# Modulation weights in pieces of two k-tiles by 512 columns, multiplied by c and added onto an accumulator in PSUM

## The reference, cut to what matters

```python
c_act = jax.nn.silu(c)
for i in range(2):
    mod = (c_act @ ada_w[i] + ada_b[i])[:, None, :]      # ada_w[i] is 1024 x 6144
    sh1, sc1, g1, sh2, sc2, g2 = jnp.split(mod, 6, axis=-1)
    h = rmsnorm_2(x, norm1_g[i]) * (1.0 + sc1) + sh1
    ...
```

## Time and profile before

| | |
|---|---|
| median of 3 runs | 3760.74 us (3753.86 to 3760.88) |
| span of the profiled execution | 3739.3 us, 40173 instructions (its time with what lies around the span is not listed) |
| PE (TensorE matmul) busy | 3177.2 us, 85% |
| DVE (VectorE) busy | 2209.4 us, 59% |
| POOL (GpSimd) busy | 2107.5 us, 56% |
| ACT (ScalarE) busy | 733.7 us, 20% |
| chain that ended last, by engine | PE 59%, DVE 21%, DVEq 9%, issue 5% |
| mean granted TensorE clock | 0.916 of full speed |
| HBM | 255.92 MB read, 69 GB/s over the span |

### The profile page before, as it was taken

One profiled execution on the slowest core, in us unless ns is written; L12 is line 12 of the kernel. 1 busy time (PEld: TensorE's weight loads), 2 busy tenths in 40 slices (PEclk: granted clock), 3 DMA queues, 4 the chain that ended last, 5 costly groups with the idle time before them and its releaser, 6 DMA issues.

```text
span 3739.3 us, 40173 instructions
## 1 busy us (share of the span) xinstructions
PE 3177.2 (85%) x14739; PEld 2448.1 (65%) x14739; DVE 2209.4 (59%) x2245; ACT 733.7 (20%) x1069; POOL 2107.5 (56%) x926
## 2 busy tenths in 40 slices
PE   7886898999779877778777998999989786699998
PEld 6775898789337755566665644677767544467776
DVE  5675654232332497777787554588338667538841
ACT  2253222432330001000000354111010111111100
POOL 5551322765018854566665502688867454368985
PEclk9897999999889987888888999999999898899999
DMA  3110000222002334444444100233222100023332
GB/s 101 56 57 29 1 0 0 79 75 72 0 0 89 120 113 129 117 116 127 132 135 121 57 0 12 79 90 90 93 66 78 59 28 15 23 68 90 90 100 69
DMA packets 365367, 259.46 MB, mean 69 GB/s; under 512 B 6330, under 2 KB 362263, under 8 KB 365005
## 3 DMA queue, kind: packets, MB, share of 16 engines
q1 hardware_dynamic: 361568, 248.53, 22.3%
q0 software_dynamic: 2256, 6.55, 0.6%
q10 hardware_dynamic: 1436, 2.96, 0.2%
HBM read 255.92 MB, written 2.10 MB: 69 GB/s over the span
## 4 chain that ended last, share of the span: by engine, by line
PE 59%; DVE 21%; DVEq 9%; issue 5%; ACT 3%; POOL 2%; POOLq 1%; DMA 1%; ACTq 0%
PE ps L487 13%; PE ps L488 13%; PE ps L489 13%; DVE adw L750 6%; DVEq L749 4%; DVE cv L1863 3%; PE ps L1364 2%; PE ps L1440 2%; PE ps L1344 2%; PE ps L1137 1%; PE ps L1150 1%; PE ps L578 1%; DVEq L2293 1%; PE ps L1247 1%; DVE SG L2247 1%
## 5 line engine op out<-in xcount | busy, mean ns | idle before, releaser
L659 POOL TENSOR_TENSOR spl<-raw,ones 128x1024 fp32r<-128x1024 f32 (+1 forms) x352 | 927.2, 2634 | 813.2 <-PE ps L489 732.3
L487 PE MATMUL ps<-HNH,spl 128*128 128x512 f32 (+1 forms) x2496 | 940.4, 377 | 121.2 <-DVE HNL L591 28.5
L661 POOL TENSOR_TENSOR spl<-raw,spl 128x1024 fp32r<-128x1024 f32 (+1 forms) x352 | 940.4, 2672 | 52.8 <-issue 3.8
L488 PE MATMUL ps<-HNL,spl 128*128 128x512 f32 (+1 forms) x2496 | 914.7, 366 | 0.0
L489 PE MATMUL ps<-HNH,spl 128*128 128x512 f32 (+1 forms) x2496 | 910.7, 365 | 0.0
L487 PEld LDWEIGHTS ps<-HNH,spl 128*128 128x128 f32 x2496 | 492.2, 197 | 243.2 <-issue 94.2
L488 PEld LDWEIGHTS ps<-HNL,spl 128*128 128x128 f32 x2496 | 493.1, 198 | 71.0 <-issue 4.3
L489 PEld LDWEIGHTS ps<-HNH,spl 128*128 128x128 f32 x2496 | 490.6, 197 | 74.0
L750 DVE TENSOR_TENSOR adw<-adw 128x512 f32<-128x512 f32 x192 | 266.8, 1390 | 14.3
L487 PE MATMUL ps<-AFH,spl 128*128 128x512 f32 x528 | 216.6, 410 | 5.3 <-issue 4.2
L2144 DVE SCALAR_TENSOR_TENSOR H<-ps,mod,H 128x512 f32<-128x512 f32 x32 | 24.0, 751 | 323.1 <-PE ps L489 323.1
(11 more groups left out here) (424 smaller groups left out, 5042.1 us busy)
## 6 DMA issues: line engine op xcount, KB each, us to landing
adw<-in_ada_w SPq DMA_DIRECT2D x96, 512.0 KB, 4.1
raw<-in_w_in SPq DMA_DIRECT2D x44, 1024.0 KB, 5.2
raw<-in_ffn_w_up SPq DMA_DIRECT2D x88, 512.0 KB, 4.7
raw<-in_w_ffn_in SPq DMA_DIRECT2D x44, 512.0 KB, 5.3
raw<-in_ffn_w_down SPq DMA_DIRECT2D x16, 1408.0 KB, 6.4
raw<-in_hy_w_in SPq DMA_DIRECT2D x12, 1024.0 KB, 5.1
raw<-in_w_ffn_out SPq DMA_DIRECT2D x8, 1408.0 KB, 7.7
raw<-in_w_branch_dn SPq DMA_DIRECT2D x8, 1024.0 KB, 5.1
```

Source lines behind the costliest of these rows:

```text
L487: pe.matmul(dst, w[0], x[0], start=first, stop=False)
L488: pe.matmul(dst, w[0], x[1], start=False, stop=False)
L659: pool.tensor_tensor(hi, w, heads_of(ones[:, :], gm.kt), ALU.mult)
L661: pool.tensor_tensor(lo, w, hi, ALU.subtract).then_inc(split_ready, 1)
```

## The change

A unit is now a piece of two k-tiles by 512 columns, again 512 KB, and four units in a row (a block) make up four columns of `mod`: 128 partitions x 8 k-tiles x 512 columns. For each of the two k-tiles VectorE does one instruction over 512 elements: it multiplies the weights by one value of silu(c) per partition and adds them onto an accumulator in PSUM (bank 5 or 7, in turn); the block's first only multiplies, and its last writes the sum to `ads` in SBUF. TensorE reduces four times 128 columns at the end of a block, behind one wait. VectorE waits for the reduction of two blocks before ahead of the block's last instruction. VectorE's loop over the slabs of `ffn_in` is written out (`turns_of`), those of the other engines stay loops. `ads` has two buffers of 512 elements in place of four of 128.

```diff
-        adw = fresh("adw", 2, KD, P)
-        ads = fresh("ads", 4, P)
+        adw = fresh("adw", 2, 2, SEQ)
+        ads = fresh("ads", 2, SEQ)
...
+        def turns_of(gm):
+
+            return [(n, range(min(R, gm.nslab - n * R))) for n in range(-(-gm.nslab // R))]
...
-        ada_w = A["ada_w_2"].rearrange("l (k p) n -> l p k n", p=P)
+        ADA_K = 4
+        ADA_BLOCKS = ADA // ADA_K
+        ada_w = A["ada_w_2"].rearrange("l (q k p) n -> l q p k n", p=P, q=ADA_K)
...
         def ada_load(sp, i, c):
 
+            j, q = c // ADA_K, c % ADA_K
             if c >= 2:
-                sp.wait_ge(ada_sum, i * ADA_TURN + (c - 1))
-            sp.dma_start(adw[:, c % 2, :, :], ada_w[c % 2][:, :, ds((i * (ADA_TURN // 2) + c // 2) * P, P)]).then_inc(ada_in[c % 2], 16)
+                sp.wait_ge(ada_used, i * ADA_TURN + (c - 1))
+            sp.dma_start(adw[:, c % 2, :, :], ada_w[j % 2, q, :, :, ds((i * (ADA_TURN // 8) + j // 2) * SEQ, SEQ)])\
+                .then_inc(ada_in[c % 2], 16)
 
         def ada_dve(dve, i, c):
 
+            j, q = c // ADA_K, c % ADA_K
+            acc = ps[:, 5 + 2 * (j % 2), :]
             dve.wait_ge(ada_in[c % 2], i * (16 * ADA_TURN // 2) + 16 * (c // 2 + 1))
-            dve.wait_ge(ada_red, i * ADA_TURN + (c + 1))
-            w = adw[:, c % 2, :, :]
-            dve.tensor_tensor(w, w, wide(csil[:, :]), ALU.mult)
-            for n in (4, 2):
-                dve.drain()
-                dve.tensor_tensor(w[:, 0:n, :], w[:, 0:n, :], w[:, n:2 * n, :], ALU.add)
-            dve.drain()
-            dve.tensor_tensor(ads[:, c % 4, :], w[:, 0, :], w[:, 1, :], ALU.add).then_inc(ada_sum, 1)
+            for h in range(2):
+                k = 2 * q + h
+                w, scale = adw[:, c % 2, h, :], csil[:, k:k + 1]
+                if k == 0:
+                    ins = dve.tensor_scalar(acc, w, scale, None, ALU.mult)
+                else:
+                    dve.drain()
+                    if k == KD - 1:
+                        dve.wait_ge(ada_red, i * (ADA_TURN // ADA_K) + (j + 1))
+                    ins = dve.scalar_tensor_tensor(ads[:, j % 2, :] if k == KD - 1 else acc, w, scale, acc, ALU.mult, ALU.add)
+            ins.then_inc(ada_used, 1)
 
         def ada_pe(pe, i, c):
 
-            pe.wait_ge(ada_sum, i * ADA_TURN + (c + 1))
-            n = i * (ADA_TURN // 2) + (c % 2 * 6 * KD + c // 2)
-            pe.matmul(ps[:, 4, ds(n, 1)], ads[:, c % 4, :], ones[:, 0:1], start=True, stop=True).then_inc(ada_red, 1)
+            if c % ADA_K == ADA_K - 1:
+                j = c // ADA_K
+                pe.wait_ge(ada_used, i * ADA_TURN + (c + 1))
+                for m in range(4):
+                    n = i * (ADA_TURN // 2) + (j % 2 * 6 * KD + j // 2 * 4 + m)
+                    mm = pe.matmul(ps[:, 4, ds(n, 1)], ads[:, j % 2, m * P:(m + 1) * P], ones[:, 0:1], start=True, stop=True)
+                mm.then_inc(ada_red, 1)
...
-            for i, slabs in groups(dve, ffn_in):
+            for i, slabs in turns_of(ffn_in):
                 for r in slabs:
                     for c in ada_units(ffn_in, r):
                         ada_dve(dve, i, c)
```

More of the change, by code:

```diff
@@ L353, in build @@
         ada_in = [sem(f"ada_in{r}") for r in range(2)]
-        ada_sum, ada_red = sem("ada_sum"), sem("ada_red")
+        ada_used, ada_red = sem("ada_used"), sem("ada_red")
         wab_split, n_y, n_hi = sem("wab_split"), sem("n_y"), sem("n_hi")
@@ L994, in _ @@
             pe.sem_inc(vt_ready, 4)
-            pe.sem_inc(ada_red, 4)
+            pe.sem_inc(ada_red, 2)
             pe.sem_inc(l2_sum, 2)
@@ L2166, in _ @@
             add_residual(ffn_out, before=lambda t: with_ada(ffn_out, t))
-            dve.wait_ge(ada_red, 4 + ADA)
+            dve.wait_ge(ada_red, 2 + ADA_BLOCKS)
             dve.tensor_tensor(mod[:, :, :].rearrange("p l n -> p (l n)"), ps[:, 4, 0:ADA], cols("ada_b", 0, ADA), ALU.add)
```

## The result

| | before | after |
|---|---|---|
| median of the runs, us | 3758.72 (3753.86 to 3760.88, 4 runs) | 3544.67 (3535.97 to 3557.47, 4 runs) |
| profiled execution, span | 3739.3 | 3534.9 |
| mean granted clock | 0.916 | 0.938 |
| VectorE busy in the five stages, us | 614.1 | 342.4 |

The ratio is 0.9433, 95% interval 0.9403 to 0.9463. The forecast was 3555, range 3528 to 3632.

A forecast was written before the change was run, and what follows sets the result against it. VectorE, taking turns with GpSimd, was held to set the pace in the five GEMM stages. Span 3739.3 less 206.0 saved there plus 21.4 around it gave 3555 us, range 3528 to 3632.

The forecast's parts named there:

- turns with GpSimd: In the five GEMM stages, VectorE instructions with two SBUF inputs and GpSimd's splits run one at a time, not together.
- rival 1: New products: PSUM as output does not free VectorE from the turns; 77 us more, 3632; chance 0.10.
- 130 to 160: Sign of being right: the new VectorE instructions are busy for 130 to 160 us in place of 472.
- rival 2: TensorE's clock stays at 0.86 in three GEMMs (ffn_in, ffn_out, mix_out); 53 us more, 3608; chance 0.06.
- Pieces done at 38: gate_sb: VectorE finishes the last two pieces 38 us into the stage.
- 21 us for the splits: gate_sb, after the pieces: 16 split instructions, 5 behind GpSimd at 2.6 us and 11 at 0.69.
- 2 us for late pieces: ffn_out: pieces that come late add 2 us to the stage's forecast of 133.
- The reductions: TensorE's reductions of units stay: 44 units add 9 or 10 us in ffn_in, 24 add 5 in ffn_out.
- rival 3: Loads: only one piece is under way, 10.0 us each; 182 us more, 3943; chance 0.05 with others on its side.
- TensorE's wait for four pieces, VectorE's for the reduction: At block ends: TensorE's 24 waits and VectorE's wait for the reduction of two blocks before cost nothing.
- 21.4 us "around the span": Whole kernel: the median of the runs before lay 21.4 us above the profiled span, and this was kept.
- The model of the turns: Own times of instructions taking turns, added per slab or tile: ffn_in 356 us, where 370.2 was measured before.

The follow-up runs named there:

- e1: The changed kernel with its accumulator in SBUF in place of PSUM, and one wait moved: 3668.82 us, ratio 0.9777.
- e2: The kernel before, its pieces and waits kept, but each unit done as eight products of 128 columns onto PSUM: 3579.96 us, ratio 0.9544.
- e7: The changed kernel with branch_sb's product and sum written to PSUM, where the split reads them: 3527.59 us, ratio 0.9414.
- e4: The changed kernel, loading only 32 of a piece's 512 columns from the third piece on: 3544.82 us, ratio 0.946.
- e6: The changed kernel with the eight splits of QSK moved in between gate_sb's pieces, two per slab: 3531.07 us, ratio 0.9415.
- e8: The changed kernel with the edits of e5, e6 and e7 together: 3474.72 us, ratio 0.9266.
- e5: The changed kernel with the first two convolution taps of both conv FFNs kept in PSUM bank 5: 3504.42 us, ratio 0.9345.
- e3: The kernel before, with TensorE's reductions in ffn_in one slab later: 3737.82 us, ratio 0.9955.

## Why the prediction was right

*The cause.* VectorE set the pace by its turns with GpSimd, and the products leave the turns because their accumulator lies in PSUM. e1 and e2 show it from both sides: the place of the accumulator is worth 124 us of 214 when taken away from the new arithmetic, and 179 when given to the old pieces. The two add to more than 214 because the new arithmetic also shortens the turns where they stay. That PSUM as an output alone is enough, which no row of before showed, L759 shows (739 to 754 ns, where the same instruction into SBUF in e1 went up to 3444): rival 1 falls. The Trainium skill, "SBUF — State Buffer", section "Who interferes with whom", has the rule that a VectorE instruction with at most one SBUF input and outside the two-port modes does not contend with GpSimd; all 192 of the new instructions agree (at most 757 ns), e1's 192 in SBUF show the other case (up to 3568 ns).

*The new instructions.* Taken at 0.75, measured 0.747 to 0.755; 144.6 us busy for "130 to 160".

*The stages.* The forecast for each and what it took: gate_sb 59, 56.7; branch_sb 57, 59.7; mix_out 63, 60.7; ffn_in 260, 258.7; ffn_out 133, 131.1. In all 206.0 less was forecast and 211.1 came. To take TensorE as the next bound, and to size it by the same GEMM elsewhere, was right to 1 or 2 us in ffn_in and ffn_out. TensorE's clock came back in both large stages (0.99 and 1.00): rival 2 falls. Some of the small misses have names, that of mix_out (2.3) has none:
- branch_sb was 2.7 over: TensorE waited twice at a block's end, 3.9 and 3.5 us, for pieces that stood behind blocked instructions (e7: gone, 48.1). The prediction had the turns of L2131 and the split, but not that they delay the reduction.
- gate_sb was right by steps that were in part right. Pieces done at 38: they were done 37.4 us in (1291.97 less 1254.6). 21 us for the splits: 19. That the last pieces are late by SP's order was in the text; that the size of the load matters was not so (e4: a sixteenth of the bytes, 0.3 us).
- ffn_out's 2 us for late pieces are not shown: e4 gains 1.7, but e6 to e8 with whole loads take 129.9 to 130.0 as well, and so differ from the kernel after by 1.2 without touching this stage.
- The reductions were added up slightly low: 44 units at 0.24 are 10.6 us, not 9 or 10, and 24 are 5.8, not 5.

*Loads and rival 3.* A piece landed in 5.0 us in the median, under the 6.0 from which the slower case would decide, and two were under way. e4 shows that the bytes have no price here, with 3.5 us of landing left.

*TensorE's wait for four pieces, VectorE's for the reduction.* 7.4 us and none, as costed, but for branch_sb.

*The mis-sized terms.* First the 21.4 us "around the span". In the profiled execution after, 2.2 us lie outside the span (3537.13 and 3534.9), and 2.2 to 3.3 in each of the other runs. The 21.4 was not time around the span: the profiled execution of before was a quick one among runs that spread (3737.64 to 3766.87 in 13 later ones). After, the median is 9.8 above the profiled span. So the term was 11.6 too large. The forecast span was 3533.3, 1.6 below the measured one, and the two together make the median's forecast 10.0 too high. That the forecast is this close owes something to luck: the stages differ by up to 2.7 us in both directions.
Second, what no step named. Outside the five stages the profiled run lost 6.7 us of its gain (3739.3 less 3534.9 is 204.4, not 211.1): the part ahead of them ended 6.1 us earlier, and the first conv FFN took 11.9 longer (fc_in 267.6, fc_out 135.3, for 265.2 and 125.8). The table shows the same GEMMs at two lengths, 125.8 or 134 to 135, 259 or 265 to 271, in kernels that do not differ there, before's included. In e5, without turns in that place, both conv FFNs have one length (250.0 and 250.1, 125.0 and 124.9) and the runs lie within 0.3%. The long fc_out has a sign: TensorE waits 7.1 us for AFL at its start and the clock is 0.96 to 0.97 (the kernel after, e1, e3, the second block of e2), where the short one has 0.5 us of that wait and 1.00, and e5 none. So VectorE's last splits come late there, and the turns are the likely reason, since they and the unevenness go together in e5. A profile of one run can hold 10 us of it. What tips it, and why the first part ended between 1250 and 1261 us in kernels that are alike there, stays open.

*The model of the turns.* The sum of own times gave before's 370 as 356, and the right order of things. It is not a way to size a case: e1 was forecast at 300 to 315 in ffn_in and took 353.4, because the sum leaves out the time in which both engines wait for TensorE. One split for each VectorE instruction that takes part, while GpSimd has work, is what the order of time shows. In the forecast the error sits in branch_sb (55 by this sum), and in rival 1's price, 311 for ffn_in and 3632 in all: e1, whose products do take turns, took 3669, so the upper end of the range was too low for the case that it stood for. The rest of the forecast did not hang on it, as the products no longer take part in any turn.

## What to carry to other kernels

Where VectorE and GpSimd both work from SBUF, look at the longest and shortest time of each VectorE line: here a factor of three and more at one shape was a turn lost. A PSUM bank as accumulator or stopover ended that in four kernels (the change, e2, e5, e7) for every instruction moved there. The price of the turns goes by the number of such instructions, up to the number that GpSimd has to do beside them, and not by their lengths; and what the stage then takes has to be followed through TensorE as well. A wait that names a line (here the reduction, 144 us) says who was late, not what is lost: removing the wait gave 14 us in its stage, removing the cause 111.

## What the runs showed of the hardware that was not expected

- While GpSimd had splits to do, each VectorE instruction with two SBUF inputs behind a drain waited for one of them: four products of 0.75 us in 11.22 us.
- A free cast from SBUF took 0.41 to 0.43 us for 512 fp32 columns, from PSUM 0.692; a free tensor_scalar from SBUF to SBUF 0.48, into PSUM 0.75. What is quicker when free was slower at the median under turns (the casts of MG in the kernel after: 1.44). The Trainium skill, "VectorE: DVE Perf Modes", section "Why PSUM operands drop a tier", says that the faster mode for fp32 needs both of VectorE's SBUF read ports, so that an operand in PSUM rules it out; these durations agree.
- 512 KB in runs of 2 KB in place of 512 B landed no sooner (medians: 5.0 us after and 4.4 in e1 with the long runs, 4.1 before and 4.0 in e2 with the short), and with a sixteenth of the bytes in 3.5 (e4).
